# Attention heads in pairs on two halves of the output partitions

## What is computed

```python
for L in range(2):
    h = layer_norm(x) * (1 + scale) + shift               # latents and context
    z = h @ w_in                                          # q, k, v of three groups, gates
    # 6 grouped-query heads (64 wide, 2 key heads), 4 differential heads (two maps each, 32 wide),
    # 6 latent-attention heads (64 + 32 rotary), values 64 wide everywhere
    p = softmax(q @ k.T * scale); o = p @ v               # latents read all 768 tokens,
    # differential: o = rms_norm(o1 - lam * o2) * gain    # context reads the 256 context tokens
    x = layer_norm(alpha * x + gate * ((o * silu(g)) @ w_out)) * ln_g + ln_b
```

## Time and profile before

| | us |
|---|---|
| median of 3 runs | 1128.35 |
| profiled execution, its own time | 1133.72 |
| its span (first to last instruction) | 1131.9 |
| TensorE matmuls busy | 1020.0 (90%) |
| VectorE busy | 555.1 (49%) |
| ScalarE busy | 406.4 (36%) |
| GpSimd busy | 316.2 (28%) |
| granted TensorE clock, mean | 0.942 |
| attention loop of layer 0, first scores to last gate | 264.6 |
| attention loop of layer 1 | 217.8 |

### The profile page before, as it was taken

The page is one execution under the profiler, slowest core; times in us unless marked ns, Lnnn a source line. Parts: engine busy times, 40 slices in busy tenths (PEclk is TensorE's granted clock), DMA queues, the critical chain, the costliest instruction groups (busy, mean ns, idle before and its releaser), DMA issues.

```text
span 1131.9 us, 12643 instructions
## 1 busy us (share of the span) xinstructions
PE 1020.0 (90%) x4527; PEld 712.2 (63%) x4527; DVE 555.1 (49%) x925; ACT 406.4 (36%) x765; POOL 316.2 (28%) x265
## 2 busy tenths in 40 slices
PE   4799999997999999999798179899979999999893
PEld 2478767985565465656687169789855545565573
DVE  5419131234444557651239856541644455763237
ACT  2522122324445355534310062232344455554320
POOL 2227222442021000001254436343622011010264
PEclk8799999996999999999999589899969999999897
DMA  9756441207312210010631112122263221001321
GB/s 364 255 172 219 165 165 39 75 30 168 85 46 50 54 29 15 16 63 1 223 112 56 56 47 66 56 72 74 66 140 70 56 56 39 21 16 57 149 75 74
DMA packets 46989, 101.63 MB, mean 90 GB/s; under 512 B 10024, under 2 KB 17136, under 8 KB 44880
## 3 DMA queue, kind: packets, MB, share of 16 engines
q1 hardware_dynamic: 45488, 95.58, 28.3%
q10 hardware_dynamic: 1440, 5.24, 1.1%
HBM read 71.33 MB, written 5.26 MB: 68 GB/s over the span
## 4 chain that ended last, share of the span: by engine, by line
PE 74%; DVE 11%; POOL 4%; SPq 3%; ACT 3%; DMA 3%; issue 2%; POOLq 0%; ACTq 0%; DVEq 0%
PE banks L837 16%; PE banks L660 13%; PE banks L661 12%; PE banks L662 12%; PE banks L816 9%; PE banks L793 5%; SPq L492 3%; PE banks L671 2%; DMA area_g<-in_w_ada_dram 2%; DVE stats L1225 1%; DVE area_b L1432 1%; PE banks L834 1%; DVE negmax L1338 1%; PE banks L850 1%; PE banks L724 1%
## 5 line engine op out<-in xcount | busy, mean ns | idle before, releaser
L1338 DVE TENSOR_REDUCE negmax<-banks 128x1 f32<-128x768 f32 (+1 forms) x200 | 169.5, 850 | 185.8 <-PE banks L793 148.4
L660 PE MATMUL banks<-w_split,area_a 128*128 128x512 f32 (+3 forms) x624 | 236.3, 379 | 16.9 <-DVE area_a L1498 10.1
L837 PE MATMUL banks<-area_z,vals 128*65 128x512 f32 x480 | 246.4, 602 | 0.9 <-ACT area_z L1030 0.5
L661 PE MATMUL banks<-w_split,area_a 128*128 128x512 f32 (+3 forms) x624 | 233.2, 374 | 0.0
L662 PE MATMUL banks<-w_split,area_a 128*128 128x512 f32 (+3 forms) x624 | 232.6, 373 | 0.0
L1135 POOL TENSOR_TENSOR w_split<-w_raw,w_split 128x512 fp32r<-128x512 f32 (+4 forms) x124 | 145.8, 1182 | 262.3 <-ACT w_split L936 262.3
L1030 ACT ACTIVATE area_z<-banks 128x512 f32<-128x512 f32 x260 | 150.8, 594 | 146.0 <-PE banks L816 144.3
L936 ACT ACTIVATE w_split<-w_raw 128x512 fp32r<-128x512 f32 (+4 forms) x124 | 70.2, 585 | 285.2 <-PE banks L662 285.1
L816 PE MATMUL banks<-area_a 96*128 96x512 f32 (+6 forms) x532 | 167.3, 411 | 3.9 <-DMA area_a<-m_row 3.6
L660 PEld LDWEIGHTS banks<-w_split,area_a 128*128 128x128 f32 x624 | 119.8, 192 | 49.1 <-issue 16.4
L662 PEld LDWEIGHTS banks<-w_split,area_a 128*128 128x128 f32 x624 | 119.5, 192 | 19.1
(11 more groups left out here) (133 smaller groups left out, 1077.6 us busy)
## 6 DMA issues: line engine op xcount, KB each, us to landing
area_g<-in_w_ada_dram SPq DMA_DIRECT2D x16, 1024.0 KB, 5.2
w_raw<-in_w_in_dram SPq DMA_DIRECT2D x32, 512.0 KB, 3.7
area_a<-parts SPq DMA_DIRECT2D x54, 192.0 KB
area_g<-in_w_ada_dram SPq DMA_DIRECT2D x16, 512.0 KB, 5.1
w_raw<-in_w_out_dram SPq DMA_DIRECT2D x16, 512.0 KB, 4.1
area_a<-parts SPq DMA_DIRECT2D x72, 96.0 KB
area_b<-in_x_dram SPq DMA_DIRECT2D x8, 512.0 KB, 9.6
x_mid<-area_b ACTq DMA_DIRECT2D x6, 512.0 KB, 2.6
```

The source lines that it names most:

```text
L660: nc.tensor.matmul(dst, a[0], b[0], start=first, stop=False)
L661: nc.tensor.matmul(dst, a[0], b[1], start=False, stop=False)
L837: mm = nc.tensor.matmul(banks[0:65, 5, :], vals[:, step, vh, :], pr, start=(step == 0), stop=(step == TILES - 1))
L1338: nc.vector.tensor_reduce(negmax[:, n % 2, t:t + 1], src, AX.X if t < CT else AX.XY, ALU.max, negate=True).then_inc(max_read, 1)
```

## The change

Two neighbouring units form a pair, and the pair is the unit of the loop: 3 grouped-query pairs (0 to 2), 4 differential (3 to 6, one head each), 3 latent-attention (7 to 9).

- Values lose the column of ones. Both heads' mix products go to one bank: the first head to output partitions 0 to 63, the second to 64 to 127. One copy, and one transpose of 128 rows for each tile, serve both.
- The denominators come from sums of the probability tiles: GpSimd adds tiles 0 to 4, VectorE tile 5 and, in layer 0, the two halves of the context tile; then TensorE multiplies each block of 128 queries (as the stationary side) by a column of ones, one column of output for each tile and head.
- Eight probability tiles (before: three) and four score banks (before: three); the maxima have banks 4 and 5 to themselves; for pair 0 they use three pairs of banks.
- The maxima run a pair and a half ahead: in pair p's turn, the last of pair p + 1 and the first six of pair p + 2. Latent-attention heads are built for pair p + 3 (products, copies, rotations) and p + 2 (high and low parts), both heads of a pair in one turn.
- Operands have fixed places instead of four slots; keys of the two key heads are loaded once a layer.
- SyncE waits for the last low part of the compressed rows before its first load of the loop, and loads heads 10 to 13 in one block in pair 3's turn.

The core of the diff:

```diff
+NP = 4
+EARLY = 6
...
+                sp.wait_ge(free_dve, N_FREE_DVE[compressed_blocks(L)[-1]])
+                sp.wait_ge(split_lo, N_SPLIT[L, 0])
+                load_keys(L, 0)
+                load_unit(L, 0)
+                load_unit(L, 1)
+                load_keys(L, 1)
+                for p in range(-1, NPAIR):
+                    for u in {-1: (2, 3), 0: (4, 5), 1: (6, 7), 2: (8, 9), 3: (10, 11, 12, 13), 5: (14, 15),
+                              6: (16, 17), 7: (18, 19)}.get(p, ()):
+                        load_unit(L, u)
+                    if p + 1 < NPAIR:
+                        load_maxrow(L, p + 1)
...
+            return 2 * (i % 3) if p == 0 else 4
...
+                    for u in range(2):
+                        mm = nc.tensor.matmul(banks[64 * u:64 * u + 64, 6, :], vals[:, step, value_head(2 * p + u), :],
+                                              prob(L, p, step, u), start=(step == 0), stop=(step == TILES - 1))
...
+                for t in q_tiles(L):
+                    for u in range(2):
+                        s = ctx_sums[:, p % 2, u, t * P:(t + 1) * P] if t < CT else total(p, u)[:, (t - CT) * P:(t - CT + 1) * P]
+                        at = 256 + 2 * (t - t0) + u
+                        mm = nc.tensor.matmul(banks[:, 7, at:at + 1], s, ones_c[:], start=True, stop=True)
...
+                for p in range(1, NPAIR):
+                    scores(L, p, 0)
+                    max_tile(L, p + 1, 6)
+                    scores(L, p, 1)
+                    max_tile(L, p + 1, 7)
+                    if context:
+                        mix(L, p - 1, "ctx")
+                    else:
+                        mix(L, p - 1, 4)
+                        mix(L, p - 1, 5)
+                    scores(L, p, 2)
+                    max_tile(L, p + 1, 8)
+                    scores(L, p, 3)
+                    turn_output(L, p - 1)
+                    denominators(L, p - 1)
+                    mix(L, p, 0)
+                    turn_max(L, p + 1)
+                    max_tile(L, p + 2, 0)
+                    mix(L, p, 1)
+                    max_tile(L, p + 2, 1)
+                    if head_pair(p + 3):
+                        mla_head(L, 2 * p + 6)
+                    scores(L, p, 4)
+                    max_tile(L, p + 2, 2)
+                    scores(L, p, 5)
+                    max_tile(L, p + 2, 3)
+                    mix(L, p, 2)
+                    max_tile(L, p + 2, 4)
+                    if head_pair(p + 3):
+                        mla_head(L, 2 * p + 7)
+                    mix(L, p, 3)
+                    max_tile(L, p + 2, 5)
+                    if context:
+                        scores(L, p, "ctx")
+                        mix(L, p, 4)
+                        mix(L, p, 5)
...
+                for p in range(1, NPAIR):
+                    exponent(L, p, 0)
+                    if context:
+                        copy_latents(L, p - 1)
+                    if head_pair(p + 2):
+                        mla_high(L, 2 * p + 4)
+                    exponent(L, p, 1)
+                    if context:
+                        copy_context(L, p - 1)
+                    else:
+                        copy_latents(L, p - 1)
+                    if head_pair(p + 2):
+                        mla_high(L, 2 * p + 5)
+                    exponent(L, p, 2)
+                    exponent(L, p, 3)
+                    copy_maxrow(L, p + 1)
...
+            def sum_probs(L, p, step):
...
+                    first = prob(L, p, 0, u) if step == 1 else total(p, u)
+                    nc.gpsimd.tensor_tensor(total(p, u), first, prob(L, p, step, u), ALU.add).then_inc(pool_summed, 1)
...
+                    if p < NPAIR:
+                        sum_probs(L, p, 2)
+                    if p and not diff:
+                        gate(L, p - 1)
+                    if p < NPAIR:
+                        sum_probs(L, p, 3)
+                    if diff:
+                        root(("diff", L, p - 1), slice(0, TILES))
+                    if p < NPAIR:
+                        sum_probs(L, p, 4)
...
+                for p in range(1, NPAIR + 1):
+                    diff = (L, p - 1) in N_NORMED
+                    reduce_max(L, p + 1, 6)
+                    if context:
+                        sum_context(L, p - 1, 0)
+                    reduce_max(L, p + 1, 7)
+                    if context:
+                        sum_context(L, p - 1, 1)
+                    reduce_max(L, p + 1, 8)
+                    if head_pair(p + 2):
+                        mla_low(L, 2 * p + 4)
+                    output_rows(L, p - 1)
+                    reduce_max(L, p + 2, 0)
+                    if head_pair(p + 2):
+                        mla_low(L, 2 * p + 5)
+                    if diff:
+                        diff_squares(L, p - 1)
+                    reduce_max(L, p + 2, 1)
+                    if diff:
+                        diff_var(L, p - 1)
+                    reduce_max(L, p + 2, 2)
+                    reduce_max(L, p + 2, 3)
+                    if p < NPAIR:
+                        sum_last(L, p, 0)
+                    reduce_max(L, p + 2, 4)
+                    if p < NPAIR:
+                        sum_last(L, p, 1)
+                    reduce_max(L, p + 2, 5)
+                    if diff:
+                        diff_norm(L, p - 1)
+                    if head_pair(p + 3):
+                        mla_rope(L, 2 * p + 6)
+                        mla_rope(L, 2 * p + 7)
```

More of the change, by code:

```diff
@@ L527, in load_unit @@
[L527 to L541 removed]
+                    r = slice(32 * ((u - 6) % 4), 32 * ((u - 6) % 4) + 32)
@@ new lines, in scores @@
+            def scores(L, p, step):
+                todo = [(kt, slice(0, NCTX), kt * NCTX) for kt in range(CT)] if step == "ctx" else [(step, lat, 0)]
+                passes = PASSES[pair_family(p)]
+                if step == 0:
+                    pe.wait_ge(mrow_in, 32 * (PN[L, p] + 1))
+                for u in range(2):
+                    r = N_RINGB["s", L, p, step, u] - 1
+                    ring_ready(r)
+                    f = operands(2 * p + u)
+                    for kt, cols, at in todo:
+                        for i, (kf, qf, rows) in enumerate(passes):
+                            mm = nc.tensor.matmul(banks[:, r % NP, at:at + cols.stop - cols.start],
+                                                  f[kf][0:rows, kt * P:(kt + 1) * P], f[qf][0:rows, cols],
+                                                  start=(i == 0), stop=(i == len(passes) - 1))
+                    mm.then_inc(ring_filled, 1)
@@ new lines, in attend @@
+                for i in range(len(max_tiles(L))):
+                    max_tile(L, 0, i)
+                turn_max(L, 0)
+                for s in range(4):
+                    scores(L, 0, s)
+                    max_tile(L, 1, s)
+                max_tile(L, 1, 4)
+                mix(L, 0, 0)
+                max_tile(L, 1, 5)
+                mix(L, 0, 1)
+                max_tile(L, 1, 6)
+                scores(L, 0, 4)
+                max_tile(L, 1, 7)
+                scores(L, 0, 5)
```

717 lines of the change are left out of this document (415 added, 302 removed).

## The result

The changed kernel is slower. Its median is 1203.3 us against 1128.1 us, ratio 1.067 [1.064, 1.070]. That is 75 us more, where the prediction had 22 us more and a range that ended at 1175 us. One of the four executions took 1488.3 us, at a granted clock of 0.63 where the other three had 0.89 to 0.90, and the ratio leaves it out.

What follows compares the result with a forecast made beforehand. TensorE bounds the loops, with VectorE close behind in building pairs and the maxima's cycle as key. Layer 0 unchanged (264.3 us) and layer 1 +22.7 make +22, a median of 1150 us; own range 1135 to 1168, full range 1097 to 1175.

Steps and rivals of the forecast that it cites:

- The halves: Mix steps: two heads on two output halves take 1.05 instead of 1.72 us, gaining 4.7 (layer 1: 4.0) us a pair.
- Maximum 7 of a building pair: Pairs 5 to 7: its matmul waits behind both rotations until 6.3 us (layer 1: 8.2) instead of 2.1.
- The two pair times by which the prediction was to be wrong: Signs of error: pairs 5 to 7 under 27 us in layer 1, or plain pairs of layer 0 under 20.
- the walk: Step-by-step timing of each pair: plain 22 us (layer 1: 19 to 19.7), building 31.3 us (30.6).
- I take 0.06: Denominators on TensorE: 0.06 us for each of 24 (16) hardware matmuls, 1.4 us (1.0) a pair.
- the far bound: Denominators: upper price from transposes of full blocks, 0.11 us each, at most 2.7 us a pair.
- the cycle of the maxima: Attention loops: a maximum may follow its forerunner after 1.66 us at the earliest; this spends most of the halves' gain.
- (b): Building pairs: TensorE's stands lower the clock, two spells for each of six pairs, 17 us more: 1167 us; chance 0.11.
- The port turns: VectorE steps with two SBUF inputs take turns with GpSimd, costing 0 to 1.3 us each.
- (a): Loops: the walk's waits overlap, each pair costs its busier engine plus a microsecond or two: 1095 us; chance 0.28.
- (c): Mix steps: the two halves don't run together, +40 to +60 us, 1180 us; chance 0.04.
- (d): Gains of 4 us a plain pair and losses in the building pairs cancel: 1128 us; chance 0.07.

Runs made afterwards that it cites:

- e6: Changed kernel with both heads of a pair writing the same half of the output partitions, one after the other: 1286.8 us, ratio 1.141.
- e1: Changed kernel with one product of 12 (layer 1: 8) ones columns in place of the 12 (8) one-column denominator products: 1154.3 us, ratio 1.022.
- e11: Kernel before the change, with VectorE's maxima reading 2 x 16 of 2 x 384 columns, waits kept: 1118.0 us, ratio 0.988.
- e3: Changed kernel with VectorE's maxima reading 2 x 16 of 2 x 384 columns, waits kept: 1161.1 us, ratio 1.027.
- e4: Changed kernel with the same denominator products spread over several places, nothing left out: 1192.9 us, ratio 1.055.
- e10: Changed kernel with spread denominators and moved rotations together, nothing left out: 1174.6 us, ratio 1.037.
- e7: Changed kernel with added 512-column matmuls that nothing reads, placed where TensorE stands: 1194.2 us, ratio 1.060.
- e13: e10 with added matmuls that nothing reads, where TensorE still stands: 1187.7 us, ratio 1.052.
- e2: Changed kernel with GpSimd's eight additions a pair cut to 16 of 512 columns, waits kept: 1204.4 us, ratio 1.066.
- e9: Changed kernel with one denominator product, maxima of 2 x 16 columns and rotations of 16 columns at once: 1087.5 us, ratio 0.962.
- e5: Changed kernel with the two heads' rotations moved to separate, other places in VectorE's order, nothing left out: 1194.1 us, ratio 1.058.
- e12: Kernel before the change, with 6 (layer 1: 4) unread one-column products added behind each head's output transposes: 1173.2 us, ratio 1.039.

## Why the prediction was wrong

**What held.** The order of things did. A mix step takes 1.01 us against 1.05. The halves earn 84 us against 10 x (4.7 + 4.0) = 87, which is partly luck: ahead of a maximum a step saves 1.86 - 1.01 = 0.85 us and not 0.67, some of it would be lost to waits, and e6 ran with 47 us less at half clock. Maximum 7 of a building pair is late by the rotations, at 5.9 us (in layer 1 at 7.7, against 8.2). Pair 3's 28 transfers took 19.8 us against 21, and TensorE stood for the row behind them 1.6 us in layer 1 and not at all in layer 0 (2.5 and 0.6). The two pair times by which the prediction was to be wrong (under 27 and under 20 us) both lie on the fast side, so neither could show that the walk was too short.

**The step that failed most clearly: "I take 0.06" for a one-column matmul.** It measures 0.112 us, the far bound. The match was a row of transposes whose stationary block has 128 columns as well. But their weight loads are not alike, first five of the transposes in the kernel before, then the denominators in the one after:

```profile
498.29 0.39 PEld L850 LDWEIGHTS banks<-ident,o_t 65*128 65x128 f32 x5 [0.29 <-issue]
```

```profile
339.71 0.97 PEld L961 LDWEIGHTS banks<-ones_c,late_bias 128*128 128x128 f32 x8
340.61 1.91 PEld L961 LDWEIGHTS banks<-ones_c,w_raw 128*128 128x128 f32 x16
```

The transposes' loads start 0.063 us apart, the denominators' 0.112 us. The time is the load's and not the moving column's: with 12 columns a hardware matmul took 0.11 us too (e1). What makes the one slower, its 128 rows instead of 65 or that it isn't a transpose, was not tried. The transposes of full blocks, the far bound, start 0.108 us apart (339.17 to 339.82, six), but that settles nothing: they have 128 moving columns where the others have 65, and at the pace of the one-head mix products before (512 columns in 0.43 us) an estimate for 65 columns is 0.055 us and for 128 columns 0.107. That 0.112 lies at this bound may be chance. (24 + 16) x 10 x 0.052 us are 21 us of the 53 by which the forecast was short.
The Trainium skill (TensorE: Matmul & The Clock Gate, LDWEIGHTS) gives a weight load as its columns divided by 1.2, in ns, whatever the rows: 107 for 128 columns. By that rule the denominators' loads agree, at 112 ns, and the transposes' don't, at 63 ns; for these the measurement decides.

**The second: the cycle of the maxima.** 1.66 us was taken, 1.73 is seen. Of TensorE's own work in it, a maximum between two mix steps is 0.55 us, not 0.35. Of the 160 maxima 54 start 1.70 to 1.78 us after their forerunner (four to seven in a plain pair, one or two in most building ones); 0.07 us in each are 4 us. The chain was in the walk, rightly; e11 and e3 put its share of the change at 30 us.

**The third: the clock, which the sum left out and rival (b) priced too narrowly.** (b) had 12 spells, only in building pairs, after stands. There were 26, eleven of them in pairs 5 to 7, and half of the time lies in other pairs, where the walk had short stands only; in the first plain pairs of layer 0 the denominators' dense stretch is enough (e4, e1). What a microsecond at 1.2 GHz costs can be read where two kernels have the same instructions in a pair. This is mix 0 of pair 3 to mix 0 of pair 4 of layer 0, in e10 and in e4 (they differ in rotations, which this pair does not have), and then mix 0 of pair 2 to that of pair 3 in layer 1, in the changed kernel and with moved rotations:

```profile
359.20:385.80 26.60, 23.50 (x100) 14.95 (x99) 13.23 (x16) 8.63 (x17) 14.16 (x11) 0.80 0.25 59
```

```profile
363.70:385.50 21.80, 18.70 (x102) 10.96 (x101) 12.41 (x16) 8.50 (x17) 12.04 (x10) 1.00 0.30 72
```

```profile
929.40:950.00 20.60, 18.34 (x80) 9.18 (x80) 9.76 (x12) 8.41 (x16) 14.80 (x11) 0.92 0.14 34
```

```profile
934.50:953.70 19.20, 16.83 (x78) 8.76 (x77) 9.76 (x12) 8.41 (x16) 14.76 (x11) 1.00 0.15 37
```

By the matmuls' own starts these are 4.9 us for 10.7 us at half clock, and 1.3 us for 3.4: 0.39 to 0.46 us for each. What brought the clock down in the first of them is open: up to the fall, at 375 in e10, TensorE's starts and stands since mix 0 are the same in both kernels to 0.02 us, a stand of 1.0 us for the maximum row among them, and in e4 the clock stayed. The 70 us outside pairs 5 to 7 so cost 27 to 32 us, less the 7 to 9 us that the 19 us before had cost. With 21 and 4 us this makes 43 to 50 of the missing 53. That the sum nearly closes doesn't prove it, since the building pairs' 65 us at half clock are not in it, and the walk's waits there may have been too long in exchange. Their price stays open. If all of it were on the path it would be another 25 to 30 us; e7, which took away 57 us of half clock for 7 us, and e13 say that much of it isn't.

**Terms that were right in kind and harmless.** The port turns (0 to 1.3 us each) happen as priced, at 1.41 instead of 0.68 us, and e2 shows that those with GpSimd's additions cost nothing. The walk had put maximum 5 behind such a turn, at a sum of 1.5 to 2 us; in the plain pair above it keeps its 1.72 us (351.79 to 353.51), and the sum after GpSimd's seventh addition took over 1.5 us in 7 of the 20 pairs and under 0.8 us in ten. The start was put 6 us too late: SyncE's first transfer went out at 258.0, not 261.1, and the first scores came at 278.4, not 284.

**Where the time went.** Halves -84. Denominators +50. Maxima +44 - 14 = +30. Rotations +28 at most, since the share that the kernel before paid is not measured. Outside the loops +8. That leaves 43 us of the 75 which no single edit shows. Most of them lie in pairs 3 to 7. With denominators, maxima and rotations all away (e9) plain pairs of layer 0 are 3.6 and 4.8 us shorter than in the kernel before with short maxima, as the halves promise, but in layer 0 pair 4 to 5 takes 24.9 us against 23.5, and in layer 1 22.5 against 19.9. The order in which two heads are built at once is a likely cause, by the waits that e5 uncovered; that is argued, not shown. It can't be the only one: from pair 3 to 4, where no head is built yet, e9 takes 23.0 us against 21.9 and 20.1 against 17.9. There it has 10 and 7 us at half clock, and TensorE's weight load stands 2.4 and 2.9 us for the maximum row, which waits behind pair 3's 28 transfers; no run has those transfers apart.

**The rivals.** (a), 1095 us, fell: it needed maximum 7 before 4 us in pair 5. (c) fell by e6; the strips that spoke against it stand in the earlier trace rows, not in rows 5 as the prediction says. (b) named a right cause, too small and in too few places; with the 0.112 us its time would have been 1167 + 21 = 1188. (d) needed gains of 4 us in plain pairs; from mix 0 to mix 0 those of layer 0 had grown by 0.5 to 2.5 us instead, and one of layer 1 had shrunk, by 0.6.

## What to carry to other kernels

A matmul with one moving column costs its weight load, here 0.11 us for a block of 128 rows and 128 columns: count weight loads, not moving columns, and look for a form in which few loads serve. Spread such matmuls among long ones (12 us here). Before giving an engine's gain away to a new order, take each suspected cost to nearly zero on its own; here the one gain of 84 us was real, and costs of 159 us stood against it, 43 of them traced to no single edit.

## What the runs showed of the hardware

Two heads' matmuls on two halves of the output partitions start 5 to 8 ns apart and take 1.01 us where one after the other takes 1.86 (e6, ahead of a maximum). A maximum's matmul between two such steps takes 0.55 us instead of 0.35. The clock fell in or within 2 us of fourteen of twenty dense stretches of one-column matmuls (2.7 us, in layer 1 1.8 us), and not at the other six. In the kernel before it did not fall at 38 of 40 stretches of 1.3 us and less (e12; the other two end the loops), and it did not fall in two plain pairs of layer 0 when the 24 were split up (e4).
